# Half-length chains for the Fourier transform, on sums and differences formed beside the input projection

## The reference, cut to what matters

```python
def fourier_branch(hmod, w_in, w_out):
    """Per channel group: Re(DFT2 over (positions, group channels)), SiLU-gated, then linear map."""
    b, n, _ = hmod.shape
    u, z = jnp.split(hmod @ w_in, 2, axis=-1)          # 1024 -> 2 x 2048
    ug = u.astype(jnp.float32).reshape(b, n, FOURIER_GROUPS, FOURIER_GROUP_DIM)   # 8 groups of 256
    f = jnp.fft.fft2(ug, axes=(1, 3), norm='ortho').real
    y = f.reshape(b, n, D_INNER).astype(hmod.dtype) * jax.nn.silu(z)
    return y @ w_out
```

## Time and profile before

| what | value |
|---|---|
| median of 3 runs | 1242.74 us (1241.93 to 1243.95) |
| the profiled execution's own time | 1242.56 us |
| its span | 1240.8 us |
| TensorE matmul busy | 1184.6 us, 95% |
| TensorE weight load busy | 1101.8 us, 89% |
| VectorE busy | 868.0 us, 70% |
| ScalarE busy | 610.1 us, 49% |
| mean granted TensorE clock | 0.983 of full speed |

### The profile page before, as it was taken

How to read it: one execution, slowest core, us unless ns; L and a number is a source line. 1 busy time by engine, 2 the same in 40 slices (tenths; PEclk the granted TensorE clock), 3 DMA queues, 4 the chain that set the end, 5 groups by cost and what they waited for, 6 DMA issues and landing times.

```text
span 1240.8 us, 22838 instructions
## 1 busy us (share of the span) xinstructions
PE 1184.6 (95%) x9234; PEld 1101.8 (89%) x9234; DVE 868.0 (70%) x1452; ACT 610.1 (49%) x981; POOL 159.6 (13%) x127
## 2 busy tenths in 40 slices
PE   6999999999999999999999899999899789999996
PEld 3777889888889999999999899999799778999996
DVE  5795874568789767655489687664678977866644
ACT  4432654467664455652543544453456655444433
POOL 0000000000000000002003313210009930231000
PEclk8999999999999999999999999999999889999998
DMA  9847321333222355442544455555423124555550
GB/s 387 348 181 274 134 69 69 132 106 133 103 99 108 136 189 205 168 131 82 191 170 141 166 176 196 174 199 174 167 102 137 68 82 153 176 201 171 194 178 34
DMA packets 28900, 195.59 MB, mean 158 GB/s; under 512 B 3464, under 2 KB 3728, under 8 KB 6416
## 3 DMA queue, kind: packets, MB, share of 16 engines
q1 hardware_dynamic: 27776, 191.90, 43.1%
q10 hardware_dynamic: 1040, 2.50, 0.6%
HBM read 193.33 MB, written 1.05 MB: 157 GB/s over the span
## 4 chain that ended last, share of the span: by engine, by line
PE 80%; DVE 10%; ACT 5%; DMA 2%; issue 1%; POOL 1%; SPq 0%; ACTq 0%; DVEq 0%
PE ps L479 23%; PE ps L480 23%; PE ps L481 23%; DVE acc L2366 3%; PE ps L829 2%; PE ps L504 2%; DVE w_lo L1716 2%; DMA ada_room<-in_weights 1%; PE ps L522 1%; DVE w_lo L1713 1%; PE ps L816 1%; PE ps L651 1%; ACT x_hi L1420 1%; DMA ring<-in_weights 1%; PE ps L872 1%
## 5 line engine op out<-in xcount | busy, mean ns | idle before, releaser
L1716 DVE TENSOR_TENSOR w_lo<-ring,w_hi 128x1024 fp32r<-128x1024 f32 x266 | 328.6, 1255 | 160.6 <-ACT w_hi L1119 153.9
L1119 ACT ACTIVATE w_hi<-ring 128x1024 fp32r<-128x1024 f32 x284 | 294.9, 1055 | 295.1 <-PE ps L481 208.8
L479 PE MATMUL ps<-x_hi,w_hi 128*128 128x258 f32 (+1 forms) x1216 | 346.4, 285 | 7.6 <-DVE x_lo L2090 4.1
L480 PE MATMUL ps<-x_lo,w_hi 128*128 128x258 f32 (+1 forms) x1216 | 344.3, 283 | 0.0
L481 PE MATMUL ps<-x_hi,w_lo 128*128 128x258 f32 (+1 forms) x1216 | 343.8, 283 | 0.0
L479 PEld LDWEIGHTS ps<-x_hi,w_hi 128*128 128x128 f32 x1216 | 231.0, 190 | 11.0 <-issue 10.8
L480 PEld LDWEIGHTS ps<-x_lo,w_hi 128*128 128x128 f32 x1216 | 231.3, 190 | 0.1
L481 PEld LDWEIGHTS ps<-x_hi,w_lo 128*128 128x128 f32 x1216 | 231.0, 190 | 0.0
L479 PE MATMUL ps<-g_hi,w_hi 128*128 128x256 f32 x608 | 171.8, 283 | 3.2 <-DVE zf L2214 1.2
L480 PE MATMUL ps<-g_lo,w_hi 128*128 128x256 f32 x608 | 170.7, 281 | 0.0
L481 PE MATMUL ps<-g_hi,w_lo 128*128 128x256 f32 x608 | 170.7, 281 | 0.0
(11 more groups left out here) (363 smaller groups left out, 1950.3 us busy)
## 6 DMA issues: line engine op xcount, KB each, us to landing
ring<-in_weights SPq DMA_DIRECT2D x148, 1024.0 KB, 4.9
o_sb<-in_weights SPq DMA_DIRECT2D x10, 1024.0 KB, 6.9
ada_room<-in_weights SPq DMA_DIRECT2D x10, 1024.0 KB, 8.5
ring<-in_weights SPq DMA_DIRECT2D x8, 512.0 KB, 4.2
ring<-in_weights SPq DMA_DIRECT2D x8, 448.0 KB
V<-in_weights SPq DMA_DIRECT2D x3, 1024.0 KB, 24.3
dft<-in_dft ACTq DMA_DIRECT2D x1, 1026.0 KB, 7.4
X<-in_x SPq DMA_DIRECT2D x1, 1024.0 KB, 4.9
```

The source lines that it names most:

```text
L479: mm(dst, w_h, x_h, start=start, stop=False, skip_group_check=True)
L480: mm(dst, w_h, x_l, start=False, stop=False, skip_group_check=True)
L1119: do(w_hi[:, q % 2, part], ring[:, q % RING, part], ACT.Copy).then_inc(S("hi_ready"), 1)
L1716: v.tensor_tensor(w_lo[:, q % 2, part], ring[:, q % RING, part], w_hi[:, q % 2, part], ALU.subtract).then_inc(S("lo_ready"), 1)
```

## The change

The transform of 256 points is split once by hand in each direction. With a and b the two halves of the positions (or of the channels), even frequencies are a transform of a + b over 128 points and odd frequencies one of a - b. So:

- In slots 0 to 7 of `fin` ScalarE no longer writes the rounded u, but adds the shift in place, to fp32 (`u_shifted`). VectorE then forms sums and differences of the halves of positions and of channels (`fold_group`, four tensor_tensor of 256 elements, through `zf` as scratch), ScalarE rounds the result to `g_hi` in one copy of 512 elements (`u_rounded`), and VectorE subtracts in one instruction of 512.
- `channels(g)` has 12 matmuls of 132 columns in place of 258: each of the two channel halves now gives its own frequencies instead of being summed with the other. `positions(g)` has 12 of 132 and 6 of 66 in place of 260 and 130.
- The table keeps 3 x 132 elements for each partition (2052 before); its load is 3 x 256 elements.
- Even and odd frequencies stand apart in PSUM. The moves out of it put them back in natural order by writing or reading SBUF with a step of two. The multiplication of the mirrored half and that of row 0 become two instructions each.
- The rounding of the gated result to `g_hi` moves from VectorE to ScalarE, two groups later in its program; the last two come before `fout`.

```diff
@@ PE
                 for n in range(2):
+                    columns = by_parity(ps[:, 2 * (g % 2) + n, :])
                     for k in range(2):
-                        last = triple(ps[:, 2 * (g % 2) + n, 0:DFT_C],
-                                      [a[:, 2 * g + k, n * P:(n + 1) * P] for a in (g_hi, g_lo)],
-                                      [a[:, k, 0:DFT_C] for a in dft_parts], k == 0, k == 1)
+                        last = triple(columns[:, k], [a[:, 2 * g + k, n * P:(n + 1) * P] for a in (g_hi, g_lo)],
+                                      [a[:, 0:2, k] for a in dft_parts], True, True)
...
                 for n in range(2):
-                    triple(dst, [a[:, g % 2, n, 0:P] for a in pq], cosines, n == 0, False)
-                    triple(dst, [a[:, g % 2, n, DFT_H:DFT_H + P] for a in pq], sines, False, n == 1)
+                    cosines = [a[:, 0:1, n].to_broadcast([P, 2, DFT_E]) for a in dft_parts]
+                    sines = [a[:, 2:0:-1, n] for a in dft_parts]
+                    triple(columns[:, n], [a[:, g % 2, n, 0:P] for a in pq], cosines, True, False)
+                    triple(columns[:, n], [a[:, g % 2, n, DFT_W:DFT_W + P] for a in pq], sines, False, True)
@@ ACT
                     if t < 8:
-                        last = do(g_hi[:, 2 * t + b, :], product[t % 2][:, b, :], ACT.Identity,
+                        last = do(product[t % 2][:, b, :], product[t % 2][:, b, :], ACT.Identity,
                                   bias=shift_of[:, u, b:b + 1])
...
-                last.then_inc(S("u_rounded") if t < 8 else S("fin_moved"), 1)
+                last.then_inc(S("u_shifted") if t < 8 else S("fin_moved"), 1)
+                if t < 8:
+                    act.wait_ge(S("u_folded"), t + 1)
+                    do(g_hi[:, 2 * t:2 * t + 2, :], product[t % 2], ACT.Copy).then_inc(S("u_rounded"), 1)
+
+            def round_transformed(g):
+                act.wait_ge(S("f_moved"), g + 1)
+                do(g_hi[:, 2 * g:2 * g + 2, :], zf[:, 2 * g:2 * g + 2, :], ACT.Copy).then_inc(S("fy_rounded"), 1)
...
-                    do(dft_parts[0], dft[:, :, :], ACT.Copy).then_inc(S("dft_rounded"), 1)
+                    do(dft_parts[0], interleaved(dft[:, :, 0:DFT_W]), ACT.Copy).then_inc(S("dft_rounded"), 1)
...
-                    do(pq[0][:, g % 2, n, :], ps[:, 2 * (g % 2) + n, 0:DFT_C], ACT.Copy).then_inc(S("pq_rounded"), 1)
+                    do(natural(0, g, n), columns_of(g, n), ACT.Copy).then_inc(S("pq_rounded"), 1)
                 if g in (2, 3):
                     hi(STARTS["fout"] + 1, halves=(g - 2,))
+                if g >= 2:
+                    round_transformed(g - 2)
+            for g in range(GROUPS - 2, GROUPS):
+                round_transformed(g)
@@ DVE
+            def fold_group(t):
+
+                x, half = product[t % 2], zf[:, 2 * t:2 * t + 2, :]
+                dve.wait_ge(S("u_shifted"), t + 1)
+                chain.step(v.tensor_tensor(half[:, :, 0:P], x[:, :, 0:P], x[:, :, P:], ALU.add))
+                chain.step(v.tensor_tensor(half[:, :, P:], x[:, :, 0:P], x[:, :, P:], ALU.subtract))
+                chain.join()
+                chain.step(v.tensor_tensor(x[:, 0, :], half[:, 0, :], half[:, 1, :], ALU.add))
+                v.tensor_tensor(x[:, 1, :], half[:, 0, :], half[:, 1, :], ALU.subtract).then_inc(S("u_folded"), 1)
+                dve.wait_ge(S("u_rounded"), t + 1)
+                v.tensor_tensor(g_lo[:, 2 * t:2 * t + 2, :], x, g_hi[:, 2 * t:2 * t + 2, :], ALU.subtract)\
+                    .then_inc(S("fin_moved"), 1)
...
                 if t < 8:
-                    dve.wait_ge(S("u_rounded"), t + 1)
-                    for b in range(2):
-                        last = v.scalar_tensor_tensor(g_lo[:, 2 * t + b, :], product[t % 2][:, b, :],
-                                                      shift_of[:, t % 4, b:b + 1], g_hi[:, 2 * t + b, :],
-                                                      ALU.add, ALU.subtract)
-                        if b == 0:
-                            chain.step(last)
-                    last.then_inc(S("fin_moved"), 1)
+                    fold_group(t)
...
-                chain.step(v.tensor_tensor(a[:, :, DFT_H:], f[:, ::-1, DFT_H - 2:0:-1], a[:, :, DFT_H:], ALU.mult))
-                chain.step(v.tensor_tensor(a[:, :, 0:DFT_H], f[:, :, 0:DFT_H], a[:, :, 0:DFT_H], ALU.mult))
+                for n in range(2):
+                    chain.step(v.tensor_tensor(far[:, :, n], mirror_columns(g, slice(None, None, -1), n), far[:, :, n],
+                                               ALU.mult))
+                chain.step(v.tensor_tensor(near, f, near, ALU.mult))
                 chain.join(1)
-                v.tensor_tensor(a[0:1, :, DFT_H:], f[0:1, :, DFT_H - 2:0:-1], gate_row(g), ALU.mult)\
-                    .then_inc(S("f_moved"), 1)
-                dve.wait_ge(S("f_moved"), g + 1)
-                v.tensor_copy(g_hi[:, 2 * g:2 * g + 2, :], a).then_inc(S("fy_rounded"), 1)
+                for n in range(2):
+                    last = v.tensor_tensor(far[0:1, :, n], mirror_columns(g, slice(None), n)[0:1],
+                                           interleaved(gate_row(g))[:, :, n], ALU.mult)
+                    if n == 0:
+                        chain.step(last)
+                last.then_inc(S("f_moved"), 1)
```

More of the change, by code:

```diff
@@ L44 @@
 DFT_C = 2 * DFT_H
-DFT_P = DFT_H + 1
+DFT_W = DFT_H + 3
+DFT_E = DFT_W // 2
 WHOLE_ROWS = 112
@@ L286, in program @@
         U_room = sc("U", (P, 4 * (DFT_C + 3 * SEQ)))
-        dft_parts = [dft_room[:, :].rearrange("p (a k n) -> p a k n", a=2, k=2)[:, a] for a in range(2)]
+        dft_parts = [dft_room[:, 0:6 * DFT_W].rearrange("p (a s e j) -> p a s e j", a=2, s=3, e=2)[:, a] for a in range(2)]
         U = U_room[:, 0:KE * SEQ].rearrange("p (k j) -> p k j", j=SEQ)
@@ L297, in program @@
         st = tensors(third)
-        dft = st("dft", (P, 2, DFT_C + 3 * SEQ))
-        pq = [st(f"pq_{part}", (P, 2, 2, DFT_C), F32R) for part in ("hi", "lo")]
+        dft = st("dft", (P, 3, SEQ))
+        pq = [st(f"pq_{part}", (P, 2, 2, 2 * DFT_W), F32R) for part in ("hi", "lo")]
         zf = st("zf", (P, KE, SEQ))
@@ L359, in gate_row, with by_parity, interleaved, natural @@
             home = (pad_a, gated)[g // 4][0:1].rearrange("p a b -> p (a b)")[:, 2 * P * (g % 4):2 * P * (g % 4 + 1)]
-            return home.rearrange("p (b j) -> p b j", b=2)[:, :, 0:SEQ - DFT_H]
+            return home.rearrange("p (b j) -> p b j", b=2)[:, :, 0:SEQ - P]
+        def by_parity(a):
+            return a[..., 0:2 * DFT_W].rearrange("p (e s j) -> p e s j", e=2, s=2)
+        def interleaved(a):
+            return a.rearrange("p s (j e) -> p s e j", e=2)
+        def natural(part, g, n):
+            return interleaved(pq[part][:, g % 2, n, :].rearrange("p (s f) -> p s f", s=2))
+        def columns_of(g, n):
+            return by_parity(ps[:, 2 * (g % 2) + n, :]).rearrange("p e s j -> p s e j")
+        def mirror_columns(g, s, n):
+            f = by_parity(ps[:, 4 + g % 4, :])[:, n]
+            return f[:, s, DFT_E - 2 - n:0:-1] if n == 0 else f[:, s, DFT_E - 3::-1]
         def mirrored(dst, src, same=False):
@@ L933, in positions @@
                     pe.wait_ge(S("f_moved"), g - 3)
-                dst = ps[:, 4 + g % 4, 0:2 * DFT_P].rearrange("p (s j) -> p s j", s=2)
+                columns = by_parity(ps[:, 4 + g % 4, :])
                 for n in range(2):
[L936 to L939, removed]
-                    triple(dst, [a[:, g % 2, n, 0:P] for a in pq], cosines, n == 0, False)
-                    triple(dst, [a[:, g % 2, n, DFT_H:DFT_H + P] for a in pq], sines, False, n == 1)
+                    cosines = [a[:, 0:1, n].to_broadcast([P, 2, DFT_E]) for a in dft_parts]
+                    sines = [a[:, 2:0:-1, n] for a in dft_parts]
+                    triple(columns[:, n], [a[:, g % 2, n, 0:P] for a in pq], cosines, True, False)
+                    triple(columns[:, n], [a[:, g % 2, n, DFT_W:DFT_W + P] for a in pq], sines, False, True)
                 for n in range(2):
-                    last = triple(ps[0:1, 4 + g % 4, DFT_P:2 * DFT_P], [a[:, g % 2, n, P:P + 1] for a in pq],
-                                  [a[:, n, DFT_C:DFT_C + DFT_P] for a in dft_parts], n == 0, n == 1)
+                    last = triple(columns[0:1, n, 1], [a[:, g % 2, n, P:P + 1] for a in pq],
+                                  [a[:, 0, n] for a in dft_parts], True, True)
                 last.then_inc(S("f_done"), 1)
@@ L1438, in move_fin @@
                     raw_root("rms1")
-                    act.dma_start(dft[:, :, :], dft_in).then_inc(S("dft_ready"), 16)
+                    act.dma_start(dft[:, :, :].rearrange("p s j -> p (s j)"), dft_in[:, 0, DFT_C:])\
+                        .then_inc(S("dft_ready"), 16)
                     act.dma_start(vec2[:, :], vec2_in).then_inc(S("vec2_ready"), 16)
@@ L1455, in move_fin @@
                     for b in range(2):
```

(21 more changed lines are left out.)

## The result

The changed kernel takes 1270.74 us (median of 4 runs, 1269.73 to 1272.63), the kernel before 1242.34: ratio 1.0237, 95% interval 1.0225 to 1.0249. It is 28.4 us slower; 1254.2 was forecast, within 1247.5 to 1260. The sign was right, and 17 us are missing from the sum.

A forecast was written before the change was run, and what follows sets the result against it. The loop of VectorE and ScalarE in `fin` was taken to end last. Fold +15.4, table -1.4 and Fourier stage -2.4 gave +11.6 on 1242.56, so 1254.2 us, range 1247.5 to 1260.

The forecast's parts named there:

- The loop of VectorE and ScalarE ends last, and the fold adds 2.26 us a turn: Slots 0 to 7 of `fin`: turns of 7.22 and 7.69 us, over TensorE's 5.76, moving slot 8's shift by +15.4 us.
- rival B: Input slots: the fold is hidden behind matmuls, so only table and Fourier stage gains remain, 1238.8 us; chance 0.07.
- The table, -1.4: Slot 10: ScalarE's table rounding of 1.81 us becomes a copy of 396 elements at 0.45, so the turn falls by 1.4.
- Weight loads set the pace of the short matmuls: Fourier stage: loads take 0.1125 us each against 0.12 a matmul now, so halving the columns of 168 matmuls wins 1.3 us.
- rival C: Fourier stage: weight loads don't pace the short matmuls; at 81 ns the time is 1248.9 us; chance 0.08.
- Moves and tail: Fourier stage: VectorE's moves stay hidden behind TensorE, steps of two cost nothing, and the last multiplication adds 0.15 us.
- rival D: Moves in the Fourier stage: writes and reads with steps of two cost double, +6 us, so 1260; chance 0.06.
- Matmuls: Fourier stage: 168 matmuls with 128 weight columns win 1.3 us and 48 with one win 1.2 us.
- Rival E: Input slots: TensorE idles about 1.5 us a turn, the clock falls to 1.2 GHz, some +34 us, so 1288; chance 0.04.

The follow-up runs named there:

- late_fold: The changed kernel with ScalarE rounding u of slot t-1 after hi(t+2) and VectorE subtracting it after the product of slot t: 1259.12 us.
- wait_filled: The changed kernel with 16 matmuls of 256 columns into an unused bank ahead of positions(0), where TensorE stood still: 1253.33 us.
- wide_again: The changed kernel with every matmul of 132 columns streaming its columns twice (264), the second time into unused columns of the bank: 1254.41 us.
- short_no_wait: The changed kernel with the fold's round trips taken apart and three moves on ScalarE, all transform matmuls still short: 1237.27 us, ratio 0.9972 to the kernel before.
- short_chains_only: The changed kernel without the fold, slots 0 to 7 as in the kernel before: 1255.00 us.
- first_wide: The changed kernel with the columns streamed twice only in channels(0), channels(1) and positions(0): 1254.18 us.
- wide_later: The changed kernel with the columns streamed twice only in channels(2), channels(3), positions(1) and positions(2): 1255.82 us.

## Why the prediction was right and wrong

- *The loop of VectorE and ScalarE ends last, and the fold adds 2.26 us a turn*: right. Turns of 7.22 and 7.68 were read, 7.22 and 7.69 forecast; +15.3 at slot 8 for +15.4. TensorE waits 1.1 to 1.6 us ahead of each of slots 4 to 10, so rival B falls. late_fold shows that it was the waits and not the instructions.
- *The table, -1.4*: right in sum, -1.37, with some luck. The two points that the copy was drawn from (512 elements in 0.62 us, 2052 in 1.81) give 0.53 for 396 elements and not 0.45; it took 0.54, and 0.1 us of it was hidden.
- *Weight loads set the pace of the short matmuls*: right. 0.112 apart at the full clock in wait_filled, 0.1125 taken from the 16-column row. The Trainium skill's page "TensorE: Matmul & The Clock Gate" gives 81 ns for such pairs under "Back-to-back issue gap"; by that figure, the measurement differs, and rival C falls.
- *Moves and tail*: right. The tail is 1.25 us (599.14 to 600.39) for 1.29, and steps of two cost next to nothing (264 elements against 258: 0.43 us for 0.42 on VectorE, 0.41 for 0.38 on ScalarE), so rival D falls. At the full clock the stage takes 22.07 us in wait_filled, for 22.6 forecast, and the whole kernel 12.7 us more than the one before, for 11.6 forecast.
- *The step that failed is the clock of TensorE in the term "Matmuls"*. It was costed at 0.1125 and 0.036 a matmul, the full clock taken for granted. At 0.50 they are 0.213 and 0.055: 168 x 0.1005 + 48 x 0.019 = 17.8 us, and 1.2 in `fout`; measured are 40.43 - 22.07 = 18.4 us between the changed kernel and wait_filled. Rival E named the fall, with 0.04, but put it in the input slots, where TensorE idles 1.1 to 1.6 us a turn between dense matmuls and the clock stays 1.00 (window 500 to 530). The argument against E was that a wait of almost 2 us ahead of `positions` had left the clock at 1.00. That wait stood behind matmuls of 258 columns, and the change made just these short. An observation of before was carried over a condition that the change removes.

What is shown is that the pair is needed: with twice the columns (wide_again), with the wait filled (wait_filled) or with it removed (short_no_wait), the stage keeps its clock. What stays open is how much of the pair must be there, and what else decides. A wait of 0.91 us (short_chains_only) was enough and one of about 0.3 (short_no_wait) was not, but their surroundings differ in more than the wait, and short_chains_only fell only 1.9 us after it. wait_filled keeps the clock through a wait of 0.81 between its first two groups of 12 short matmuls. And at the wait of 1.29 ahead of `fout`, behind short matmuls each time, two of six traces kept it.

## What to carry to other kernels

Shortening the moving operand below the cost of a weight load wins little directly (here 3 us of a stage of 25), and waits that were harmless to the clock behind longer matmuls can then cost it: check each wait of TensorE that the shorter matmuls touch, and fill or remove it before they are made shorter. Before work is put on an engine with idle time, add up its loop with the other engine, wait by wait: here VectorE was 70% busy and had 0.33 us a turn. Where a loop in program order ends last, do the second half of a round trip one turn later.

## What the runs showed of the hardware

- The granted clock has a memory. Short matmuls (132 columns behind loads of 128 weight columns, back to back) kept 1.00 for 19 us (first_wide) and 21 us (wait_filled), and at 0.50 didn't get it back in 39 us (the changed kernel); in wide_later it was back behind 16 matmuls of 264 columns. The Trainium skill's page "TensorE: Matmul & The Clock Gate", Part 1, says that the throttled state is the default and activity releases it; here, TensorE was busy without a gap at 0.50 from 560 us to the wait ahead of `fout` (2.00 of 2.00 us in the window 560 to 562), and the clock wasn't released, so the measurement decides: a TensorE that the profile shows busy throughout can still stay at 1.2 GHz.
- At 0.50 the distance of the short matmuls is 0.213 us, 1.9 times the 0.112 at 1.00: the pace of the weight loads goes with the same clock.
- 16 useless matmuls in a wait of 1.9 us made the stage behind them 18.4 us shorter and the kernel 16 to 18 us faster.
